# Dilated projections: 13 of 18 weight pieces as seven products of half blocks, state space tables in steps between

## The chip, the cores and the metric

The kernel runs on one core of a Trainium2 chip. The metric is the device time of one execution in microseconds, as the median of several runs. All arithmetic that is spoken of here is in f32.

## The reference

Four layers on 256 tokens of 1024 columns. The first two (attention with 256 context tokens, then attention on a grid, each with a mixture of 32 experts) are not touched. The third is dilated attention with 16 heads of 64, in three groups of different window and dilation, the fourth a grouped state space layer. What the change touches is the product `h @ w_in` of the third layer:

```python
def dilated_attention_mixer(h, w_in, w_out, rel_bias):
    B, S, _ = h.shape                       # 1, 256
    proj = h @ w_in                         # 1024 x (3*3*1024 + 1024)
    n_qkv = 3 * N_GROUPS_A * ATTN_WIDTH
    qkv = proj[..., :n_qkv].reshape(B, S, 3, N_GROUPS_A, ATTN_HEADS, HEAD_DIM)
    z = proj[..., n_qkv:]
    for g, (window, dilation) in enumerate(DILATED_GROUPS):
        o, l = dilated_group_attention(qkv[:, :, 0, g], qkv[:, :, 1, g], qkv[:, :, 2, g],
                                       rel_bias, window, dilation)
    ...
    return (o * jax.nn.silu(z)) @ w_out
```

The fourth layer's decays exp(A dt), their powers and a table of cosines and sines over 64 steps are computed on the chip from small inputs; these are the "state space tables".

## The kernel before

Every engine has a program of its own, in a fixed order written out by hand, and they meet on semaphores only: `ev(kind, ...)` is a signal, `at(kind, ...)` a wait for it, `vstep` a VectorE instruction that the next one waits for. The sync engine (SP) streams the weights through a ring of slots in SBUF, in the third layer three slots of 2 MB. A slot is loaded again when the last product that reads it has ended.

The heads are done in two halves, `hh` 0 and 1. Each half has nine weight pieces of 1024x512, `("dil", hh, g, c)`, for the groups g = 0, 1, 2 and c = 0 (Q), 1 (K), 2 (V). They are cut into parts, listed in `DIL`. A part of Q or K is one block of 128 output columns for all 256 tokens: 8 matmuls with a 128x128 block of the weight standing and 256 tokens moving, which leaves the result transposed (columns on the partitions). A part of V is one block of 128 tokens: 8 matmuls with the tokens standing and 512 weight columns moving. A half has 30 parts; n = 0 to 3 are (0, Q), 4 to 7 (0, K), and so on. The last two (n = 28, 29, the V piece of group 2) and the first six of the other half run between the attention steps of `pe_pairs`.

Around them: `pe_dil_part` (L2655) writes part n into PSUM bank n % 4. `act_dil_part` copies it to SBUF (L2680 for Q with the scale 0.125, L2682 for K, L2684 for V). In the second half VectorE copies K (L2691). `act_dil` runs ScalarE's parts, and after part 3 of the first half `act_tables` (exp, exp, sine, cosine on 128x32, L2527 to L2533). VectorE does, during the first half, all of `dve_tables`: L2549 and L2550, the wrapping of the angle in `dve_wrapped` (L2537 to L2544, twice), then small instructions on 128x32 (L2555 to L2618), and the table of angles, doubled from 1 to 64 (L2580 to L2585), on 32 to 1024 columns. `dve_outputs_begin` (L2937 to L2942, six instructions of 128x1024) runs after part 7 of the second half. GpSimd does eight masks `BM` of 128x768 before each half's attention (L2825); in the first half they wait for the constant `DM`, which ScalarE's queue loads (L2795). `pe_power_rows` turns the powers for a later load. `dil_done` is the wait of every engine for the last copies, and then come the attention steps (`pe_pairs`, `act_pairs`, `dve_pairs`, `pool_pairs`).

Three other places serve as measures in the rows below: `pe_keep` (L533) multiplies the identity by itself, 128 columns moving, just to keep TensorE at work; L2159 is a turn by matmul, with 128x128 blocks of the stream standing and 128 columns moving; L2858 is GpSimd's gate product on 128x256.

## Time and profile before

| | |
|---|---|
| median of 3 runs | 2081.4 us (2079.29 to 2089.8) |
| span of the profiled execution | 2082.8 us |
| TensorE busy | 1934.9 us, 93% |
| VectorE busy | 652.8 us, 31% |
| ScalarE busy | 364.7 us, 18% |
| GpSimd busy | 322.1 us, 15% |
| L2666 (Q and K parts) | 768 records of 128x256, 168.0 us |
| L2668 (V parts) | 192 records of 128x512, 84.1 us |

Times in a trace are microseconds from the start of the span. A record is one TensorE instruction; an f32 matmul of the program is two of them. PE is TensorE's matmuls and PEld its weight loads, which run beside them; DVE is VectorE, ACT ScalarE, POOL GpSimd. "Busy" of TensorE is the union of overlapping records, so the pace of a row of matmuls is read from the time between starts, not from the length of one. Idle time in brackets stands before the row, with the engine or DMA that ended it.

### The profile page before, as it was taken

What the parts mean: (1) busy time and instruction counts of PE and PEld (TensorE: products, weight loads), DVE (VectorE), ACT (ScalarE), POOL (GpSimd) and SP (SyncE); (2) the same over time, 40 slices, a digit from 0 to 9 for tenths busy, and PEclk for the clock granted to TensorE, in tenths of its full rate; (3) what the DMA queues carried; (4) which work ended last, traced back from release to release, by engine and by line L of the source; (5) the groups of instructions that cost most, each with busy time, mean ns of one, the idle gap of its engine ahead of it and who ended that gap; (6) DMA issues with size and microseconds to landing.
All of it is one profiled execution on the core that took longest, in us unless ns stands there. A gap on an engine that the chain in (4) does not pass through costs nothing.

```text
span 2082.8 us, 33820 instructions
## 1 busy us (share of the span) xinstructions
PE 1934.9 (93%) x14647; PEld 1203.4 (58%) x14647; DVE 652.8 (31%) x1517; ACT 364.7 (18%) x809; POOL 322.1 (15%) x264
## 2 busy tenths in 40 slices
PE   6989999999999989998999988888789999989998
PEld 4565566555555555546555444444376677675884
DVE  1343472222222242115421111111154131047752
ACT  3142410000000021213210000000020220042231
POOL 0143411000000100116110000000020060040120
PEclk9999999999999999999999999999999999999999
DMA  9694499999999988217599999999874414327221
GB/s 350 157 366 165 156 365 400 427 428 426 426 426 426 427 337 237 91 59 296 212 380 426 427 427 426 426 426 426 363 276 160 157 49 161 121 82 203 82 93 61
DMA packets 136109, 590.93 MB, mean 284 GB/s; under 512 B 19410, under 2 KB 35818, under 8 KB 111248
## 3 DMA queue, kind: packets, MB, share of 16 engines
q1 hardware_dynamic: 119536, 564.45, 68.7%
q10 hardware_dynamic: 10304, 17.83, 2.7%
q0 software_dynamic: 6112, 6.39, 0.9%
q8 instruction: 118, 1.93, 0.4%
q14 instruction: 39, 0.32, 0.0%
HBM read 576.95 MB, written 25.33 MB: 289 GB/s over the span
## 4 chain that ended last, share of the span: by engine, by line
PE 67%; DMA 22%; DVE 4%; issue 3%; POOL 2%; ACT 2%; SPq 0%; DVEq 0%; POOLq 0%; ACTq 0%
DMA RG<-in_moe_w 20%; PE banks L1594 13%; PE banks L2666 8%; PE banks L1619 6%; PE banks L1139 4%; PE banks L2261 4%; PE banks L2668 4%; PE banks L1570 4%; PE banks L2263 3%; PE banks L2867 3%; PE banks L3078 2%; PE banks L712 2%; DMA mods_rows<-AR 2%; PE banks L355 2%; POOL AR L957 1%
## 5 line engine op out<-in xcount | busy, mean ns | idle before, releaser
L1594 PE MATMUL banks<-RG,HT 128*64 128x256 f32 x3616 | 426.5, 389 | 35.9 <-DMA RG<-in_moe_w 33.2
L1594 PEld LDWEIGHTS banks<-RG,HT 128*64 128x64 f32 x3616 | 252.0, 134 | 222.1 <-DMA RG<-in_moe_w 56.2
L1873 POOL DMA_INDIRECT y_rows<-AR x64 | 63.9, 998 | 838.3 <-DVE AR L1633 809.9
L1603 DVE TENSOR_TENSOR AR<-AR,banks 128x256 f32<-128x256 f32 x64 | 38.6, 603 | 479.4 <-ACT AR L1599 428.2
L1619 PE MATMUL banks<-RG,AR 128*64 128x512 f32 x752 | 171.7, 598 | 3.1 <-DVE AR L1612 3.1
L2666 PE MATMUL banks<-HT,RG 128*128 128x256 f32 x768 | 168.0, 380 | 0.8 <-ACT HT L550 0.8
L2666 PEld LDWEIGHTS banks<-HT,RG 128*128 128x128 f32 x768 | 145.4, 190 | 22.8 <-issue 2.4
L1599 ACT ACTIVATE AR<-banks 128x256 f32<-128x256 f32 x64 | 24.6, 384 | 742.3 <-PE banks L1594 742.3
L1570 PE MATMUL banks<-AR 128*128 128x256 bf16 (+1 forms) x1152 | 149.3, 277 | 1.6 <-DVE AR L1558 1.5
L1570 PEld LDWEIGHTS banks<-AR 128*128 128x128 bf16 x1152 | 108.2, 98 | 33.3 <-issue 18.3
L1619 PEld LDWEIGHTS banks<-RG,AR 128*64 128x64 f32 x752 | 49.8, 136 | 93.8 <-issue 83.6
L1139 PE MATMUL banks<-RG,HT 128*128 128x512 f32 x192 | 87.5, 617 | 4.8 <-DVE AR L405 3.0
L2261 PE MATMUL banks<-HT,RG 128*128 128x256 f32 (+1 forms) x256 | 85.3, 489 | 3.2 <-ACT HT L2181 1.3
L2668 PE MATMUL banks<-RG,HT 128*128 128x512 f32 x192 | 84.1, 594 | 0.0
L957 POOL TENSOR_SCALAR AR<-AR,ST 128x768 f32<-128x768 f32 (+1 forms) x24 | 45.0, 1886 | 242.5 <-DVE ST L935 242.4
L957 POOL TENSOR_SCALAR AR<-AR,SVT 128x512 f32<-128x512 f32 x27 | 42.0, 1566 | 190.3 <-DVE SVT L935 190.3
L2261 PEld LDWEIGHTS banks<-HT,RG 128*128 128x128 f32 x256 | 47.7, 190 | 40.7 <-issue 35.6
L1139 PEld LDWEIGHTS banks<-RG,HT 128*128 128x128 f32 x192 | 37.8, 199 | 51.8 <-issue 51.8
L1583 ACT ACTIVATE HT<-banks 128x256 f32<-128x256 f32 x128 | 49.1, 384 | 106.2 <-PE banks L1570 105.1
L355 PE MATMUL banks<-RG,SC 128*32 128x128 f32 x1536 | 51.1, 291 | 15.2 <-DMA RG<-in_ada_w 15.2
L1594 PE MATMUL banks<-AR,HT 128*64 128x256 f32 x480 | 59.1, 398 | 6.5 <-DMA AR<-in_moe_w 6.5
L878 PE MATMUL banks<-IDN,AR 128*128 128x128 f32 x348 | 52.2, 284 | 11.8 <-POOL AR L957 9.4
(487 smaller groups left out, 2381.3 us busy)
## 6 DMA issues: line engine op xcount, KB each, us to landing
RG<-in_moe_w SPq DMA_DIRECT2D x160, 2048.0 KB, 23.4
AR<-in_moe_w SPq DMA_DIRECT2D x32, 2048.0 KB, 14.5
RG<-in_ada_w SPq DMA_DIRECT2D x24, 2048.0 KB, 10.7
RG<-in_attn_w_in SPq DMA_DIRECT2D x20, 2048.0 KB, 7.7
RG<-in_odd_w_in SPq DMA_DIRECT2D x6, 2048.0 KB, 19.7
RG<-in_ssm_w_in SPq DMA_DIRECT2D x4, 2048.0 KB, 8.8
AR<-y_rows SPq DMA_DIRECT2D x12, 512.0 KB, 6.0
RG<-in_even_w_out SPq DMA_DIRECT2D x2, 2048.0 KB, 12.3
```

Source lines behind the costliest of these rows:

```text
L355: m = pe.matmul(q[32 * j:32 * j + 32, :], SC[:, k, :], w[:, k, 128 * j:128 * j + 128], start=k == 0, stop=k == 7, skip_group_check=True)
L957: g.tensor_scalar(u["pb"][x], u["pb"][x], A.small_of(s, 3)[:, x:x + 1], None, MUL).then_inc(*ev("weighed_pool", name, s, x))
L1139: m = pe.matmul(PS[b], HT[:, k, 128 * t:128 * t + 128], w[:, k, :], start=k == 0, stop=k == 7)
L1570: m = pe.matmul(p, E.HB[t][:, i, k, :], E.one_hot(g, t), start=t == 0 and i == 0, stop=t == E.nt - 1 and i == 2)
L1594: m = pe.matmul(p[64 * h:64 * h + 64, 256 * i:256 * i + 256], x[:, k, :], w[:, h, k], start=k == 0, stop=k == 7, skip_group_check=True)
L1619: m = pe.matmul(q[64 * h:64 * h + 64, :], x, w2[:, i, 512 * h:512 * h + 512], start=i == 0, stop=i == 3)
L1873: g.indirect_dma_start(y, off, E.Y[b], None, bounds_check=2047, oob_is_err=False).then_inc(*event)
L2261: m = pe.matmul(p[:, 0:wd], w[:, k, 128 * j:128 * j + 128], HT[:, k, 0:wd], start=k == 0, stop=k == 7)
L2263: m = pe.matmul(p, HT[:, k, 128 * j:128 * j + 128], w[:, k, :], start=k == 0, stop=k == 7)
L2666: m = pe.matmul(p[:, 0:256], w[:, k, 128 * j:128 * j + 128], HT[:, k, 0:256], start=k == 0, stop=k == 7)
L2668: m = pe.matmul(p, HT[:, k, 128 * j:128 * j + 128], w[:, k, :], start=k == 0, stop=k == 7)
L2867: m = pe.matmul(PS[2 * h + t], src[:, k, 128 * t:128 * t + 128], w[:, k, :], start=k == 0, stop=k == 7)
```

## The change

13 of the 18 pieces (all but (0, Q) and (2, V) in the first half, and all but (0, Q), (0, K) and (2, V) in the second) are computed with seven products of half blocks in place of eight. The weight piece is cut into four blocks b11, b12, b21, b22 of 512x256 and the input into four of 128 tokens by 512. The sums of input blocks (`dve_seven_sums`, four instructions of 128x512 on VectorE) are made once per half. The sums of weight blocks are made for each piece, each one instruction on 128x1024, in place in the slot or in a scratch tile: GpSimd makes t3 = b22 - b12 and t2 = t3 + b11, VectorE makes t1 = b22 - t2 and t4 = b21 - t2. The products go to PSUM banks 0, 1 and 4. ScalarE copies the first product ("one") and writes one quarter of the output; VectorE makes u2 and u3 and writes the other three quarters ("22", "21", "12"), each reading a bank and a small tile, on 256 columns. A product of a Q or K piece is 8 matmuls with 128 tokens moving, one of a V piece 4 matmuls with 256 weight columns moving. The slot of the ring is free after the seventh product.

VectorE's tables are cut into 28 steps for the first half, one to seven instructions each, and 13 for the second; `dve_seven` takes one at four places of each piece. Up to the argument of the cosine they run as before, ahead of the first piece. `dve_outputs_begin` moves into the first half's steps, the doublings from 16 on into the second half. ScalarE's four table instructions stand one behind each of the parts 0 to 3. GpSimd's masks stand two behind each of the first four pieces. In the second half GpSimd starts after the last attention output of the first half.

```diff
+        def dil_seven(hh, g, c):
+
+            return (g, c) not in (((0, 0), (2, 2)), ((0, 0), (0, 1), (2, 2)))[hh]
...
-                    cols(("dil", hh, g, c), AW, c * 3072 + g * 1024 + hh * 512, 512, ("dil_in", hh, g, c, 3 if c < 2 else 1))
+                    cols(("dil", hh, g, c), AW, c * 3072 + g * 1024 + hh * 512, 512,
+                         ("seven", "dil", hh, g, c, 6) if dil_seven(hh, g, c) else ("dil_in", hh, g, c, 3 if c < 2 else 1))
...
+            def __init__(self, key, before, w, turned, banks, x, sums, t2, small, scale, outs):
+                self.key, self.before, self.turned, self.scale, self.outs = key, before, turned, scale, outs
+                self.b11, self.b12 = w[:, 0:4, 0:256], w[:, 0:4, 256:512]
+                self.b21, self.b22 = w[:, 4:8, 0:256], w[:, 4:8, 256:512]
+                self.banks = [PS[b][:, 0:256] for b in banks]
+                self.t2, (self.one, self.u2, self.u3) = t2, small
+                a, b, c = self.banks
+                self.products = ((a, x[0][0], self.b11, True), (b, sums[1], t2, True), (a, x[0][1], self.b21, False),
+                                 (b, sums[2], self.b12, False), (c, sums[0], self.b11, True), (b, x[1][1], self.b21, False),
+                                 (c, sums[3], self.b22, False))
...
+        def dve_seven_sums(v, key, x, sums):
+
+            s1, s2, s3, s4 = sums
+            v.tensor_tensor(s3, x[0][0], x[1][0], SUB)
+            vstep(v, v.tensor_tensor(s1, x[1][0], x[1][1], ADD))
+            vstep(v, v.tensor_tensor(s2, s1, x[0][0], SUB))
+            v.tensor_tensor(s4, x[0][1], s2, SUB).then_inc(*ev("seven_sums", *key))
+
+        def pe_seven_product(pe, Z, i):
+            q, x, w, first = Z.products[i]
+            for j in range(2 if Z.turned else 1):
+                for k in range(4):
+                    if Z.turned:
+                        m = pe.matmul(q[:, 128 * j:128 * j + 128], w[:, k, 128 * j:128 * j + 128], x[:, k, :],
+                                      start=first and j + k == 0, stop=k == 3, skip_group_check=True)
+                    else:
+                        m = pe.matmul(q, x[:, k, :], w[:, k, :], start=first and k == 0, stop=k == 3, skip_group_check=True)
+            m.then_inc(*ev("seven", *Z.key, i))
+
+        def pe_seven(pe, Z, landed_, sums):
+            pe.wait_ge(*landed_)
+            if Z.before is not None:
+                pe.wait_ge(*at("seven_11", *Z.before))
+            pe_seven_product(pe, Z, 0)
+            pe.wait_ge(*at("seven_sums", *sums))
+            pe.wait_ge(*at("seven_t2", *Z.key))
+            if Z.before is not None:
+                pe.wait_ge(*at("seven_21", *Z.before))
+            pe_seven_product(pe, Z, 1)
+            pe.wait_ge(*at("seven_one", *Z.key))
+            pe_seven_product(pe, Z, 2)
+            pe.wait_ge(*at("seven_u2", *Z.key))
+            pe_seven_product(pe, Z, 3)
+            pe.wait_ge(*at("seven_t1", *Z.key))
+            if Z.before is not None:
+                pe.wait_ge(*at("seven_12", *Z.before))
+            pe_seven_product(pe, Z, 4)
+            pe.wait_ge(*at("seven_t4", *Z.key))
+            pe.wait_ge(*at("seven_u3", *Z.key))
+            pe_seven_product(pe, Z, 5)
+            pe.wait_ge(*at("seven_22", *Z.key))
+            pe_seven_product(pe, Z, 6)
+
+        def act_seven(act, Z):
+            act.wait_ge(*at("seven", *Z.key, 0))
+            if Z.before is not None:
+                act.wait_ge(*at("seven_21", *Z.before))
+            act.activation(Z.one, Z.banks[0], ACT.Copy, scale=Z.scale).then_inc(*ev("seven_one", *Z.key))
+            act.wait_ge(*at("seven", *Z.key, 2))
+            act.activation(Z.out(0, 0), Z.shaped(Z.banks[0]), ACT.Copy, scale=Z.scale).then_inc(*ev("seven_11", *Z.key))
+
+        def dve_seven(v, Z, fill):
+            a, b, c = Z.banks
+
+            def add(out, bank, u, event):
+                v.scalar_tensor_tensor(out=out, in0=bank, scalar=Z.scale, in1=u, op0=MUL, op1=ADD).then_inc(*ev(event, *Z.key))
+
+            next(fill, None)
+            v.wait_ge(*at("seven_t2", *Z.key))
+            v.wait_ge(*at("seven", *Z.key, 0))
+            v.tensor_tensor(Z.b11, Z.b22, Z.t2, SUB).then_inc(*ev("seven_t1", *Z.key))
+            v.wait_ge(*at("seven_one", *Z.key))
+            v.wait_ge(*at("seven", *Z.key, 1))
+            if Z.before is not None:
+                v.wait_ge(*at("seven_12", *Z.before))
+            add(Z.u2, b, Z.one, "seven_u2")
+            next(fill, None)
+            v.wait_ge(*at("seven", *Z.key, 2))
+            v.tensor_tensor(Z.b21, Z.b21, Z.t2, SUB).then_inc(*ev("seven_t4", *Z.key))
+            v.wait_ge(*at("seven", *Z.key, 3))
+            add(Z.u3, b, Z.one, "seven_u3")
+            next(fill, None)
+            v.wait_ge(*at("seven_u3", *Z.key))
+            v.wait_ge(*at("seven", *Z.key, 4))
+            add(Z.out(1, 1), Z.shaped(c), Z.shaped(Z.u3), "seven_22")
+            next(fill, None)
+            v.wait_ge(*at("seven", *Z.key, 5))
+            add(Z.out(1, 0), Z.shaped(b), Z.shaped(Z.one), "seven_21")
+            v.wait_ge(*at("seven", *Z.key, 6))
+            add(Z.out(0, 1), Z.shaped(c), Z.shaped(Z.u2), "seven_12")
+
+        def pool_seven(g, Z, landed_):
+            g.wait_ge(*landed_)
+            g.tensor_tensor(Z.b12, Z.b22, Z.b12, SUB).then_inc(*ev("seven_t3", *Z.key))
+            g.wait_ge(*at("seven_t3", *Z.key))
+            if Z.before is not None:
+                g.wait_ge(*at("seven_t4", *Z.before))
+            g.tensor_tensor(Z.t2, Z.b12, Z.b11, ADD).then_inc(*ev("seven_t2", *Z.key))
...
-        def act_tables(act):
-            act.wait_ge(*at("table_loads", 4))
-            act.activation(DT, LDT, ACT.Exp).then_inc(*ev("dt"))
-            act.wait_ge(*at("decay"))
-            act.activation(RR, V0, ACT.Exp).then_inc(*ev("radius"))
-            act.wait_ge(*at("sine_in"))
-            act.activation(SI_, V2, ACT.Sin).then_inc(*ev("sine"))
-            act.wait_ge(*at("cosine_in"))
-            act.activation(CO, V0, ACT.Sin).then_inc(*ev("cosine"))
+        def act_table(act, i):
+            if i == 0:
+                act.wait_ge(*at("table_loads", 4))
+                act.activation(DT, LDT, ACT.Exp).then_inc(*ev("dt"))
...
+        def dve_tables_rest(v):
+
             v.wait_ge(*at("cosine"))
...
             vstep(v, v.tensor_tensor(G1, AIM, AIM, MUL))
+            yield
             vstep(v, v.tensor_tensor(G0, G0, G1, ADD))
             vstep(v, v.reciprocal(G0, G0))
...
+            yield from dve_outputs_begin(v)
+            v.memset(RC[:, :, 0:1], 1.0)
+            vstep(v, v.memset(RS[:, :, 0:1], 0.0))
...
+        def dve_angles(v, s, end, once):
+
+            while s < end:
+                c, d = bc(PC, 2, s), bc(PSN, 2, s)
+                x0, y0 = RC[:, :, 0:s], RS[:, :, 0:s]
+                x1, y1 = RC[:, :, s:2 * s], RS[:, :, s:2 * s]
+                w = XS[:, 3, :].rearrange("p (a b) -> p a b", a=32)[:, :, 0:s]
+                steps = ((x1, x0, c, MUL), (w, y0, d, MUL), (x1, x1, w, SUB), (y1, x0, d, MUL), (w, y0, c, MUL), (y1, y1, w, ADD))
+                for i, (o, a, b, op) in enumerate(steps):
+                    ins = v.tensor_tensor(o, a, b, op)
+                    if 2 * s == 64 and i == 5:
+                        ins.then_inc(*ev("angles"))
+                        v.wait_ge(*at("angles"))
+                    else:
+                        vstep(v, ins)
+                    if (i + 1) % once(s) == 0:
+                        yield
+                s *= 2
+                if s < 64:
+                    dve_squared(v, PC, PSN, PC, PSN)
+                    yield
...
         DIL_EARLY, DIL_LATE = 6, 28
+        DIL_X = [[HT[:, 4 * kh:4 * kh + 4, 128 * t:128 * t + 128] for kh in range(2)] for t in range(2)]
+        DIL_SUMS = [ar(3 * KK + 512 * i, 4, 128) for i in range(4)]
+        DIL_SMALL = [ar(5 * KK + 256 * i, 256) for i in range(3)]
+
+        def dil_sevens(hh):
+            pieces, before = [], None
+            for g in range(3):
+                for c in range(3):
+                    if dil_seven(hh, g, c):
+                        if c == 2:
+                            outs = [[V3[:, t, g, 256 * b:256 * b + 256] for b in range(2)] for t in range(2)]
+                        else:
+                            o = Q3[g] if c == 0 else K3[:, g]
+                            outs = [[o[:, 2 * b:2 * b + 2, 128 * t:128 * t + 128] for b in range(2)] for t in range(2)]
+                        key = "dil", hh, g, c
+                        pieces.append(Seven(key, before, where[key][0], c < 2, (0, 1, 4), DIL_X, DIL_SUMS, ar(2 * KK, 4, 256),
+                                            DIL_SMALL, 0.125 if c == 0 else 1.0, outs))
+                        before = key
+            return pieces
+
+        SEVENS = [dil_sevens(hh) for hh in range(2)]
...
-            if (g, c, j) == (0, 2, 0) and hh:
-                act.wait_ge(*at("att_out", "dil0", 7))
...
+        def dil_plain(hh):
+
+            return range(DIL_EARLY, 8) if hh else range(4)
+
         def act_dil(act, hh):
-            for n in range(DIL_EARLY if hh else 0, DIL_LATE):
+            for n in dil_plain(hh):
                 act_dil_part(act, hh, n)
-                if hh == 0 and n == 3:
-                    act_tables(act)
+                if hh == 0:
+                    act_table(act, n)
+            if hh:
+                act.wait_ge(*at("att_out", "dil0", 7))
+            for Z in SEVENS[hh]:
+                act_seven(act, Z)
+
+        def dve_dil(v, hh):
+            v.wait_ge(*at("turned_out", "dil", 1, 1))
+            dve_seven_sums(v, ("dil", hh), DIL_X, DIL_SUMS)
+            if hh == 0:
+                dve_tables(v)
+                fill = chain(dve_tables_rest(v), dve_angles(v, 1, 16, lambda s: 2 if s == 8 else 3))
+            else:
+                for n in dil_plain(hh):
+                    dve_dil_part(v, hh, n)
+                fill = dve_angles(v, 16, 64, lambda s: 1)
+            for Z in SEVENS[hh]:
+                dve_seven(v, Z, fill)
+            run(fill)
+
+        def pool_dil(g, hh):
+            masks = iter(range(8))
+            if hh:
+                g.wait_ge(*at("att_out", "dil0", 7))
+            for Z in SEVENS[hh]:
+                pool_seven(g, Z, landed(Z.key))
+                for h in islice(masks, 2):
+                    pool_mask(g, hh, h)
+            for h in masks:
+                pool_mask(g, hh, h)
 
         def dil_done(e, hh):
 
-            e.wait_ge(*at("dil_out_act", hh, 2, 0, 3))
-            e.wait_ge(*at(*dil_out(hh, 2, 1, 3)))
+            e.wait_ge(*at("seven_11", "dil", hh, 2, 1))
+            e.wait_ge(*at("seven_12", "dil", hh, 2, 1))
...
-                for n in range(DIL_EARLY if hh else 0, DIL_LATE):
+                for n in dil_plain(hh):
                     pe_dil_part(pe, hh, n)
+                for n in (4, 5) if hh else (0, 1):
+                    pe.wait_ge(*at(*dil_out(hh, *DIL[n])))
+                for Z in SEVENS[hh]:
...
         def dve_dilated(v):
             dve_final(v)
-            dve_tables(v)
             for hh in range(2):
-                if hh:
-                    for n in range(DIL_EARLY, DIL_LATE):
-                        dve_dil_part(v, hh, n)
-                        if n == 7:
-                            dve_outputs_begin(v)
+                dve_dil(v, hh)
                 dil_done(v, hh)
...
+        def pool_mask(g, hh, h):
+            g.tensor_tensor(BM[:, h], bc(BI[:, 8 * hh + h, :], 1, 3), DM, ADD).then_inc(*ev("mask", hh, h))
+
         def pool_dilated(g):
+            g.wait_ge(*at("turned_out", "dil", 1, 1))
             g.wait_ge(*at("mask_load"))
             g.wait_ge(*at("dist_rows", 1))
             g.wait_ge(*at("finished", 1))
             for hh in range(2):
                 if hh:
                     g.wait_ge(*at("shift", "dil0", 7))
-                for h in range(8):
-                    g.tensor_tensor(BM[:, h], bc(BI[:, 8 * hh + h, :], 1, 3), DM, ADD).then_inc(*ev("mask", hh, h))
+                pool_dil(g, hh)
                 pool_pairs(g, A2[hh], iter(()))
...
-            t1, t2 = ar(2 * KK, 32, 32), ar(3 * KK, 32, 32)
+            t1, t2 = [XS[:, i, :].rearrange("p (a b) -> p a b", a=32) for i in (2, 3)]
             v.wait_ge(*at("matrix_loads", 3))
             cr, ci = bc(CR, 2, 32), bc(CI, 2, 32)
+            yield
             v.tensor_tensor(t1, C2R, ci, MUL)
+            yield
             vstep(v, v.tensor_tensor(t2, C2N, ci, MUL))
```

In `act_table(act, i)` the four instructions of `act_tables` are the same, one for each i. `dve_tables` ends where the cosine's argument is ready.

## Rows read from the trace of the kernel before

**Rows 1.** The page: engines by busy time, and the slices.

```profile
PE 1934.9 (93%) x14647; PEld 1203.4 (58%) x14647; DVE 652.8 (31%) x1517; ACT 364.7 (18%) x809; POOL 322.1 (15%) x264
...
PEclk9999999999999999999999999999999999999999
```

**Rows 2.** The chain in order of time: start us, us, what ran.

```profile
1532.56 27.89 PE banks L2666 x128
...
1643.21 0.39 ACT AR L2682
...
1721.66 13.73 PE banks L2668 x32
...
1776.76 27.64 PE banks L2666 x128
```

**Rows 3.** Timeline, TensorE, 755 to 793: start us, us, engine, line, operation, shapes.

```profile
758.58 8.20 PE L533 MATMUL banks<-IDN 128*128 128x128 f32 x72
...
785.04 3.73 PE L2159 MATMUL banks<-AR,XS 128*128 128x128 f32 x32
```

**Rows 4.** Timeline, ScalarE, 1539 to 1556.

```profile
1539.77 0.38 ACT L2680 ACTIVATE HT<-banks 128x256 f32<-128x256 f32 x1 [2.85 <-PE banks L2666]
...
1554.55 0.23 ACT L2531 ACTIVATE SVT<-SVT 128x32 f32<-128x32 f32 x1 [3.09 <-DVE SVT L2544]
```

**Rows 5.** Timeline, VectorE, 1530 to 1640.

```profile
1548.70 1.20 DVE L2549 TENSOR_TENSOR SVT<-SVT 128x32 f32<-128x32 f32 x1 [18.50 <-ACT SVT L2527]
1549.82 1.84 DVE L2550 TENSOR_TENSOR SVT<-SVT 128x32 f32<-128x32 f32 x1
1551.70 1.72 DVE L2537 TENSOR_SCALAR SVT<-SVT 128x32 f32<-128x32 f32 x1
1553.46 0.18 DVE L2538 CAST SVT<-SVT 128x32 int32<-128x32 f32 x1
...
1583.05 1.22 DVE L2580 TENSOR_TENSOR RG<-RG,SVT 128x1024 f32<-128x1024 f32 x1
```

**Rows 6.** Groups by form, VectorE: count, busy us, mean ns, idle before.

```profile
L1603 DVE TENSOR_TENSOR AR<-AR,banks 128x256 f32<-128x256 f32 x64 | 38.6, 603 | 479.4 <-ACT AR L1599 428.2 <-issue 51.2
```

**Rows 7.** Timeline, GpSimd, from 1535; the masks alone in short windows.

```profile
1539.22 14.16 POOL L2825 TENSOR_TENSOR AR<-AR 128x768 f32<-128x768 f32 x8 [39.10 <-DMA AR<-in_k_dm]
...
1549.82 1.80 POOL L2825 TENSOR_TENSOR AR<-AR 128x768 f32<-128x768 f32 x1
...
1551.58 1.80 POOL L2825 TENSOR_TENSOR AR<-AR 128x768 f32<-128x768 f32 x1
```

**Rows 8.** Groups by form, GpSimd.

```profile
L574 POOL TENSOR_TENSOR AR<-AR 128x1024 f32<-128x1024 f32 x1 | 2.4, 2353 | 1.5 <-DVE AR L561 1.5
```

**Rows 9.** Timeline, VectorE and GpSimd together, 1824 to 1878.

```profile
1824.75 5.61 POOL L957 TENSOR_SCALAR AR<-AR,ST 128x768 f32<-128x768 f32 x3 [6.66 <-DVE ST L935]
...
1826.12 0.97 DVE L928 CUSTOM_DVE_ANT_0 banks<-banks,AR 128x768 f32<-128x768 f32 x1 [1.15 <-PE banks L850]
...
1870.53 0.73 POOL L2858 TENSOR_TENSOR XS<-XS,AR 128x256 f32<-128x256 f32 x1 [4.67 <-ACT AR L2851]
...
1875.64 1.44 POOL L2858 TENSOR_TENSOR XS<-XS,AR 128x256 f32<-128x256 f32 x1 [4.38 <-ACT AR L2851]
1876.52 1.63 DVE L2952 TENSOR_TENSOR AR<-AR 128x1024 f32<-128x1024 f32 x1
```

**Rows 10.** Windows: length us, busy and count by engine, granted clock, DMA share, GB/s.

```profile
1516.00:1518.00 2.00, 0.00 (x0) 0.00 (x0) 1.97 (x2) 0.00 (x0) 0.00 (x0) 1.00 1.03 393
1518.00:1519.60 1.60, 0.00 (x0) 0.00 (x0) 1.56 (x3) 1.15 (x2) 0.00 (x0) 0.50 1.05 389
...
1524.00:1526.00 2.00, 2.00 (x16) 2.00 (x15) 1.56 (x8) 0.77 (x3) 0.00 (x0) 0.79 1.08 366
```

**Rows 11.** Timeline, TensorE, 1495 to 1521.

```profile
1519.66 1.65 PE L533 MATMUL banks<-IDN 128*128 128x128 f32 x6 [5.74 <-DVE AR L2503]
```

**Rows 12.** The page: DMA issues: count, KB each, us to landing.

```profile
RG<-in_attn_w_in SPq DMA_DIRECT2D x20, 2048.0 KB, 7.7
```

83 lines of the change are left out of this document (47 added, 36 removed).

## The prediction

> **What bounds the kernel now.** I read the page first, then the chain of waits in order of time, then single engines in short windows. The page says that TensorE is busy for 93% of the span, at the full granted clock in every slice [rows 1]. The chain through the changed stage shows one thing only: from 1532.56 on it is the projection matmuls of L2666 and L2668, piece after piece with nothing between, to 1643.21 in the first half of the heads and from 1721.66 to 1804.40 in the second [rows 2]. TensorE's own time per piece is therefore on the path at full price, and so is every wait that is put into it. No row shows the chain on VectorE, ScalarE or GpSimd there; their work hides under 111 and 83 us of matmuls. What the reader should see besides is that this cover is now spent twice: the seven-product scheme makes VectorE and GpSimd work inside each piece, with TensorE waiting for them seven times a piece.
>
> **TensorE's part.** An f32 matmul is two records in the trace. Two Q/K pieces are 128 records of 256 columns in 27.64 us, 215.9 ns each, so a piece is 64 records, 13.82 us; a V piece is 32 records of 512 columns in 13.73 [rows 2]. After, a Q/K piece is 7 products of 8 matmuls, 112 records, but of 128 columns only. Their price is that of rows with the same shape, a fresh 128x128 load for each: L533 does 72 in 8.20 us and L2159 does 32 in 3.73; less the last one's 0.27 that is 7.93/71 = 111.7 and 3.46/31 = 111.6 ns [rows 3]. So 112 x 111.6 = 12.50 us, 1.32 less. It is not half of 215.9 (12.09), and I take the row. A V piece is 7 x 4 matmuls of 256 columns, 56 records x 215.9 = 12.09 us, 1.64 less. Of the 13 pieces 9 are Q or K (five in the first half of the heads) and 4 are V: 9 x 1.32 + 4 x 1.64 = 18.4 us off the path, if nothing waits. One product is 1.79 us (Q/K) or 1.73 (V).
>
> **What the product chain asks of the others.** One product's result reaches ScalarE or VectorE 0.30 us after its last record's slot (two parts of 16 records at 215.9 ns from 1532.56 end at 1539.47, the copy of the second begins at 1539.77 [rows 4]). In a piece VectorE runs, in this order: a table step, t1 (128x1024), u2, a table step, t4 (128x1024), u3, a table step, "22", a table step, "21", "12". A 128x1024 tensor_tensor is 1.22 us; the five with a PSUM input have 256 columns, and I take 0.50 for each, under the 0.60 of L1603, whose second input is in PSUM (at 0.60 the sum is 1.5 higher) [rows 6]. GpSimd runs t3 and t2 (128x1024), then two masks. A mask is 1.77 on average (8 in 14.16), and a 128x1024 there is 2.35, in proportion to the mask's 768 columns [rows 7, 8]. Alone, this all fits: VectorE has 2.4 + 2.5 us of own work and four table steps of about 1.1 each (five steps of 32 columns at 0.225 apart), 9.3 of 12.5 us; each of TensorE's waits is met with some 1 us in hand; GpSimd has 8.2 of 12.5. The end of a half gains 0.3 us of tail, because the last product is followed by a VectorE add instead of a 0.39 us copy. That sum is -18.4 + 0.3 = about -18.
>
> **But they don't run side by side.** This is where I chose. In the trace of before the first table steps meet the masks. Three VectorE instructions of 32 columns, whose fellows take 0.18, took 1.20, 1.84 and 1.72 us, and each ended within 0.1 us of the end of a mask instruction (one starts at 1549.82, one at 1551.58, the last ends at 1553.38); from 1553.46, with GpSimd idle, they are 0.18 again [rows 5, 7]. So a VectorE instruction waits for the whole GpSimd instruction, and only one gets in between two of them, although the second was ready. It holds the other way too: L2858 takes 1.44 in place of 0.73 where a 128x1024 of VectorE runs, and VectorE's next, at 1876.52, takes 1.63 in place of 1.22 [rows 9]. With an input in PSUM VectorE is not held: L928, 768 columns, takes 0.97 inside GpSimd's three from 1824.75 [rows 9], about a column a nanosecond and no more. Thus u2, u3, "22", "21", "12" are free of it; t1, t4, the four sums and all table steps are not.
> The Trainium skill (SBUF — State Buffer, "Who interferes with whom") says the same and adds that whoever starts first keeps the shared ports for its whole instruction; had the page a bandwidth split instead, the steps of 32 columns would cost next to nothing and the sum would be the -18. The rows here side with the lock.
>
> Walk through a piece with this rule. After t4, GpSimd's t2 of the next piece is released and it runs t2, mask, mask, t3 without a gap: 2.35 + 2 x 1.77 + 2.35 = 8.2 us. VectorE's third table step stands between u3 and "22". If it is five small instructions, they get in one by one between those four, so "22" ends 8.2 + 0.5 + 0.3 us or so after t4's end. TensorE wants "22" for the seventh product two products and a half after t4, about 3 us. The stall is near 6 us. That meets pieces one and two of the first half (6.4, 6.0) and piece two of the second (6.0), whose third step is a squaring of five. Where the third step is one or two instructions it is 0 to 2.4. Laid out with the same rule for all of them, TensorE waits 3.1 (below) + 0.8 + 6.4 in piece one, 6.0 in two, 0.5 in three, 2.0 + 1.3 in four, 2.4 in five, 0.2 in six: 22.7 us. In the second half, where the steps are mostly single instructions of 512 or 1024 columns: 0.6, 6.9, 0.5, 2.1, together 10.1. The 3.1: the masks' data land at 1539.22 [rows 7], GpSimd then runs t3, t2, two masks and t3 until 1549.8, and the 16 wrapping steps behind "dt" crawl; the sine on ScalarE waits for them, and ScalarE's fourth part copy, the cosine and the copy "one" are queued behind that sine. In before the sine comes as late as 1554.55, but with 27.6 us of cover from the next piece [rows 4].
> Sum: -18.4 + 0.3 + 22.7 + 10.1 = **+14.7 us**. With 128x1024 on GpSimd a tenth shorter it is +9.6, a tenth longer +20.
>
> **The clock.** Before L533 TensorE is idle for 5.74 us, to 1519.66 [rows 11]. The granted clock is still 1.00 from 1516 to 1518 and 0.50, which is 1.2 of 2.4 GHz, from 1518 on; over 1524 to 1526 it averages 0.79, so it is back at 1524.84, 5.2 us after work begins [rows 10]. Each such fall costs half of 5.2, 2.6 us. I have three stalls of 6.0 to 6.4 us, just longer than the idle that brought it down, so 0 to 7.8 us; I take half, 3.9.
> Forecast: 2082.8 + 14.7 + 3.9 = 2101.4 for the profiled execution. The median of the runs is 1.4 below the profiled span, so **2100.0 us**, 0.9% slower.
>
> **What costs nothing.** The angle tables are wanted only in the state space stage, past 1950; the powers by power rows at the end of the first half, and they are in the second piece's steps. Weight pieces of 2 MB land 7.7 us after issue [rows 12] and there are three slots, so a piece in 12 to 20 us starves nobody. Moving ScalarE's wait for the last attention output ahead of the V pieces delays only copies that come later anyway. The masks come later than now, yet are done by the fourth piece, before the attention. Four sums of 512 columns (0.69 each) run at 1532.5, before the first seven-product piece at 1546.4.
>
> **Rivals.** (1) *The lock does not bind*: small instructions slip through, TensorE's waits stay met, 2082.8 - 18.1 - 1.4 = **2063**, 0.9% faster. The price is the 18.4 of fewer columns; it decides as long as the third table step ends before the sixth product. For it speaks that only three instructions were seen held; against it that all three were held to the end. 17%. (2) *Half of it*: the lock is there but the meeting is rarer (GpSimd held back by VectorE's own instructions, a second small one getting in, 2.1 us instructions), so the stalls are 10 to 27 us instead of 33, with no fall of the clock: **2073 to 2091**, within 0.5%. 20%. (3) *Narrow matmuls slower than L2159's*: if the recorded load of 0.19 us were the pace at 128 columns, a Q/K piece were 21.3 us, 67 us more in all, 2150 or above. L533 and L2159 speak against it. 3%. The forecast with its stalls has 60%: 2092 to 2112.
>
> **How the numbers follow.** The range for 8 in 10 leaves out rival 1 and rival 3: 2070 to 2112; the likeliest case alone is 2092 to 2112. 0.5% (10.4 us) is about what a measurement of this kernel can tell. Faster 0.19 (rival 1 and the edge of 2), same 0.19, slower 0.62 (forecast and rival 3).
>
> **What would show it.** In the changed kernel: products of 16 records in 1.79 and 1.73 us (else the first term is wrong); table steps of 32 columns at 1.8 to 2.4 us while GpSimd works (else the lock is); TensorE idle 6 us before the seventh product, released by "22", in the first two pieces; a ScalarE sine late enough to hold "one"; a clock of 0.50 in slices behind these idles. If TensorE is gapless there, rival 1 holds and I am wrong by 36 us; if the gaps are there but half as long, my count of meetings is wrong.

## The result and the profile after

The changed kernel took **2099.77 us** (median; 2096.05 to 2108.01, 5 runs) against 2081.88 of the kernel before in the same comparison (2079.29 to 2089.8, 5 runs). The ratio is 1.0078, with a 95% interval of 1.0052 to 1.0104: about 0.8% slower. The profiled execution has a span of 2099.7 us; 2082.8 was that of before.

The page of the changed kernel (busy us, share of the span, instructions; then the granted clock by slices):

```profile
PE 1924.4 (92%) x15175; PEld 1230.0 (59%) x15175; DVE 766.3 (36%) x1608; ACT 359.0 (17%) x799; POOL 392.5 (19%) x290
...
PEclk9999999999999999999999999999989999999999
```

Beside [rows 1] TensorE is busy for 10.5 us less, VectorE for 113.5 us more and GpSimd for 70.4 more. The span grew all the same, so TensorE must be waiting, and one slice shows a lower clock. Where it is can be read from two windows for each kernel: the first half of the heads, from the first projection matmul to the first attention product, and the second half, from the group of 48 projection matmuls to the first attention product behind them. TensorE alone; columns: window, length, busy (records), granted clock, DMA share, GB/s. Before:

```profile
1532.56:1643.74 111.18, 110.83 (x451) 1.00 0.47 168
1711.04:1804.99 93.95, 93.34 (x370) 1.00 0.38 135
```

After, and below them short windows around the stalls:

```profile
1535.38:1659.96 124.58, 107.88 (x738) 0.95 0.42 147
1727.25:1823.13 95.88, 87.67 (x610) 0.98 0.38 133
...
1566.00:1572.00 6.00, 3.90 (x17) 0.50 0.00 0
1580.00:1590.00 10.00, 4.95 (x19) 0.81 0.00 0
```

The two halves take 220.5 us instead of 205.1, 15.3 more. That is nearly the whole of the 16.9 by which the spans differ: another 2.8 lie ahead of the stage, where both kernels do the same work and profiled executions differ by several us, and the rest of the kernel gives 1.2 back. In the first half TensorE is idle for 16.7 us (124.58 less 107.88), where it was idle for 0.35.

TensorE's timeline in the first two pieces and around the one long stall of the second half:

```profile
1554.20 2.05 PE L1002 MATMUL banks<-HT,RG 128*128 128x128 f32 x16 [1.16 <-ACT AR L1036]
...
1560.31 1.95 PE L1002 MATMUL banks<-HT,RG 128*128 128x128 f32 x16
1568.10 3.78 PE L1002 MATMUL banks<-AR,RG 128*128 128x128 f32 x16 [5.84 <-DVE AR L1044]
...
1587.68 3.78 PE L1005 MATMUL banks<-RG,AR 128*128 128x256 f32 x8 [5.05 <-DVE AR L1044]
...
1593.89 1.95 PE L1002 MATMUL banks<-AR 128*128 128x128 f32 x16
1595.68 1.95 PE L1002 MATMUL banks<-HT,RG 128*128 128x128 f32 x16
...
1767.33 3.56 PE L1002 MATMUL banks<-AR,RG 128*128 128x128 f32 x16 [5.14 <-DVE HT L1044]
```

Before, the rows were unbroken [rows 2]. Here products follow one another in 1.79 us only where nothing disturbs them (1593.89 to 1595.68). The seventh product of pieces one and two (L1002 and L1005) waits 5.84 and 5.05 us for VectorE's "22" (L1044), then runs in 3.78 us instead of about 2, at half the clock. What VectorE did in the first of these stalls:

```profile
1558.92 0.42 DVE L1044 SCALAR_TENSOR_TENSOR AR<-banks,AR 128x256 f32<-128x256 f32 x1
1559.25 2.29 DVE L2690 TENSOR_TENSOR SVT<-SVT 128x32 f32<-128x32 f32 x1
1561.58 1.72 DVE L2691 TENSOR_TENSOR SVT<-SVT 128x32 f32<-128x32 f32 x1
1563.34 1.73 DVE L2692 TENSOR_TENSOR SVT<-SVT 128x32 f32<-128x32 f32 x1
1565.10 2.26 DVE L2693 TENSOR_TENSOR SVT<-SVT 128x32 f32<-128x32 f32 x1
1567.40 0.19 DVE L2694 TENSOR_TENSOR SVT<-SVT 128x32 f32<-128x32 f32 x1
1567.62 0.42 DVE L1044 SCALAR_TENSOR_TENSOR AR<-banks,AR 128x256 f32<-128x256 f32 x1
```

and GpSimd in the same time (t2 L1076, two masks L3000, t3 L1072):

```profile
1559.15 2.35 POOL L1076 TENSOR_TENSOR AR<-RG 128x1024 f32<-128x1024 f32 x1 [6.67 <-DVE RG L1057]
1561.46 3.56 POOL L3000 TENSOR_TENSOR AR<-AR 128x768 f32<-128x768 f32 x2
1564.97 2.34 POOL L1072 TENSOR_TENSOR RG<-RG 128x1024 f32<-128x1024 f32 x1
```

Four additions of 32 columns take as long as GpSimd's four instructions, one each, and end as those end; the fifth takes 0.19 us, GpSimd being done. The same happened to three instructions before the change [rows 5, 7], where nobody waited.

### The profile page after: what moved, and what is told of

Read it like the earlier page. It is cut to its first block, busy times and chain, and to the rows that moved or that the text cites. A ratio compares the mean times of both kernels' runs of the same rounds, so it can differ in the third digit from the quotient of the medians.

```text
span 2099.7 us, 35070 instructions
## 1 busy us (share of the span) xinstructions
PE 1924.4 (92%) x15175; PEld 1230.0 (59%) x15175; DVE 766.3 (36%) x1608; ACT 359.0 (17%) x799; POOL 392.5 (19%) x290
## 4 chain that ended last, share of the span: by engine, by line
PE 62%; DMA 22%; DVE 8%; issue 3%; POOL 2%; ACT 2%; ACTq 0%; SPq 0%; DVEq 0%; POOLq 0%
DMA RG<-in_moe_w 20%; PE banks L1710 12%; PE banks L1735 5%; PE banks L1002 4%; PE banks L1255 4%; PE banks L2377 4%; PE banks L1686 3%; PE banks L2379 3%; PE banks L3052 3%; PE banks L3270 2%; PE banks L719 2%; DMA mods_rows<-AR 2%; PE banks L1005 2%; POOL AR L964 1%; PE banks L661 1%
## 5 line engine op out<-in xcount | busy, mean ns | idle before, releaser
L1686 PEld LDWEIGHTS banks<-AR 128*128 128x128 bf16 x1152 | 108.4, 98 | 33.6 <-issue 18.3
L1255 PE MATMUL banks<-RG,HT 128*128 128x512 f32 x192 | 86.1, 609 | 4.8 <-DVE AR L412 3.0
L2377 PEld LDWEIGHTS banks<-HT,RG 128*128 128x128 f32 x256 | 47.7, 190 | 40.7 <-issue 35.6
L1002 PE MATMUL banks<-AR,RG 128*128 128x128 f32 x432 | 55.3, 287 | 13.7 <-DVE AR L1044 8.5
L1749 DVE TENSOR_TENSOR AR<-banks,XS 128x512 f32<-128x512 f32 x32 | 22.1, 691 | 115.3 <-PE banks L1735 115.3
L1735 PE MATMUL banks<-AR 128*64 128x512 f32 x272 | 62.1, 598 | 1.0 <-DVE AR L1728 1.0
L1002 PEld LDWEIGHTS banks<-AR,RG 128*128 128x128 f32 x432 | 52.8, 202 | 15.2 <-DVE AR L1044 9.7
```

The lines of the kernel that those rows point to most:

```text
L1002: m = pe.matmul(q[:, 128 * j:128 * j + 128], w[:, k, 128 * j:128 * j + 128], x[:, k, :], start=first and j + k == 0, stop=k == 3, skip_gro ...
L1255: m = pe.matmul(PS[b], HT[:, k, 128 * t:128 * t + 128], w[:, k, :], start=k == 0, stop=k == 7)
L1686: m = pe.matmul(p, E.HB[t][:, i, k, :], E.one_hot(g, t), start=t == 0 and i == 0, stop=t == E.nt - 1 and i == 2)
L1735: m = pe.matmul(q[64 * h:64 * h + 64, :], x, w2[:, i, 512 * h:512 * h + 512], start=i == 0, stop=i == 3)
L2377: m = pe.matmul(p[:, 0:wd], w[:, k, 128 * j:128 * j + 128], HT[:, k, 0:wd], start=k == 0, stop=k == 7)
```

## The experiments

The theory, **by turns**: VectorE and GpSimd instructions that both work in SBUF don't run side by side; a small one waits for the whole large one, one for each. The third table step of a piece meets GpSimd's stretch, holds "22", and with it TensorE. The rival, **load**: with the combinations of the scheme and the table steps, VectorE simply has more to do between two products than fits. A second rival came up later, **place**: a step between u3 and "22" is too much there, whatever GpSimd does.

Times are against the kernel before in the same comparison (medians there 2080.8 to 2084.4). Because profiled executions differ by several us ahead of the stage (it starts between 1527 and 1538), the surer measure is the length of the two halves, read as above, from one profiled execution of each kernel:

| kernel | first half | second | sum | median us | ratio, 95% |
|---|---|---|---|---|---|
| before | 111.2 | 94.0 | 205.1 | | 1 |
| changed | 124.6 | 95.9 | 220.5 | 2099.8 | 1.0052 to 1.0104 |
| masks_twice | 128.1 | 99.2 | 227.2 | 2109.3 | 1.0112 to 1.0148 |
| third_step_behind_22 | 117.1 | 94.6 | 211.6 | 2093.5 | 1.0026 to 1.006 |
| keep_clock | 122.1 | 94.4 | 216.5 | 2093.8 | 1.0026 to 1.0064 |
| masks_late | 120.8 | 89.6 | 210.4 | 2087.8 | 1.0 to 1.0031 |
| steps_last | 113.3 | 86.5 | 199.8 | 2084.8 | 0.9998 to 1.003 |
| weight_sums_only | 121.3 | 98.8 | 220.0 | 2092.5 | 1.003 to 1.0068 |
| weight_sums_masks_moved | 105.1 | 86.9 | 192.0 | 2070.0 | 0.9902 to 0.9949 |
| weight_sums_on_vectore | 103.9 | 86.3 | 190.1 | 2070.2 | 0.991 to 0.9947 |
| one_mask_per_piece | 101.4 | 85.4 | 186.8 | 2064.2 | 0.9888 to 0.9934 |

**masks_twice**: more of GpSimd's work, with nothing more for VectorE.

```diff
                 for h in islice(masks, 2):
+                    gstep(g, g.tensor_tensor(BM[:, h], bc(BI[:, 8 * hh + h, :], 1, 3), DM, ADD))
                     pool_mask(g, hh, h)
```

> The changed kernel with each of GpSimd's eight masks per half made twice (the first copy feeds nobody); VectorE's and TensorE's programs are untouched. If VectorE's instructions wait for whole GpSimd instructions (the lock), the stretch behind t4 grows from t2, mask, mask, t3 = 8.2 us to t2, four masks, t3 = 11.8 us, and the five-instruction third steps meet five of them in place of four: about 14 us more than the changed kernel, near 2114 us. If TensorE waits only because VectorE has too much of its own to do, nothing changes, since GpSimd is idle for 7 to 12 us in each piece: 2100 us.

Measured: 6.7 us more in the two halves than the changed kernel, half of the 14 expected. A new stall of 4.72 us came up (the third product, for the copy "one"), and the three stalls behind "22" became shorter, not longer: 4.29, 2.99 and 4.33 us, which the theory as it stood did not say. VectorE's third step of piece one, and GpSimd beside it (L2878 the added copies):

```profile
1563.58 1.51 DVE L2690 TENSOR_TENSOR SVT<-SVT 128x32 f32<-128x32 f32 x1
1565.12 1.73 DVE L2691 TENSOR_TENSOR SVT<-SVT 128x32 f32<-128x32 f32 x1
1566.89 0.19 DVE L2692 TENSOR_TENSOR SVT<-SVT 128x32 f32<-128x32 f32 x1
1567.11 1.68 DVE L2693 TENSOR_TENSOR SVT<-SVT 128x32 f32<-128x32 f32 x1
```

```profile
1565.00 1.81 POOL L2878 TENSOR_TENSOR AR<-AR 128x768 f32<-128x768 f32 x1
1566.88 1.86 POOL L3001 TENSOR_TENSOR AR<-AR 128x768 f32<-128x768 f32 x1
1568.70 1.80 POOL L2878 TENSOR_TENSOR AR<-AR 128x768 f32<-128x768 f32 x1
```

A second small instruction (L2692) gets in at 1566.89, where GpSimd has waited for the end of its own added copy before it starts the mask (from about 1566.81 to 1566.88). The step also began later, with GpSimd's t2 already under way, so that its first addition was held for 1.51 us and not 2.29. Load says 2100 and is out; the rule needs the correction that such a gap on GpSimd lets a second small one through.

**third_step_behind_22**: the third step's place alone.

```diff
             add(Z.u3, b, Z.one, "seven_u3")
-            next(fill, None)
             v.wait_ge(*at("seven_u3", *Z.key))
             v.wait_ge(*at("seven", *Z.key, 4))
             add(Z.out(1, 1), Z.shaped(c), Z.shaped(Z.u3), "seven_22")
             next(fill, None)
+            next(fill, None)
```

> The changed kernel with VectorE's third table step of each piece behind the addition 22 in place of ahead of it; the work of every engine is the same. If the place in VectorE's queue is what turns a held table step into an idle TensorE, the 6 us idles ahead of the seventh product go, and smaller ones (about 4 us, behind 21, which the next piece's second product wants) take their place: laid out with the same rule it is 13 us less, about 2087 us. If the amount of work or of lock time is what counts, it stays at 2100 us.

Measured: 8.9 us less in the two halves, 6.3 less in the median, where 13 were expected. The same four additions (L2690 to L2693) now take 0.62, 1.73, 1.73 and 2.27 us behind "22", and hold "21" instead, on which the next piece's second product waits: 3.75 and 2.85 us of idle in the first half, 3.16 in the second. The clock still fell behind them (the product after the first of these waits took 2.52 us and the next 3.07 in place of 1.89). The hold went on, only its victim changed.

**keep_clock**: the price of the clock by itself. TensorE multiplies the identity ahead of the seventh product in the three pieces with a long stall; nothing reads the result.

```diff
+            if Z.key[1:] in ((0, 0, 1), (0, 0, 2), (1, 1, 0)):
+                pe_keep(pe, 16, 5)
             pe.wait_ge(*at("seven_22", *Z.key))
             pe_seven_product(pe, Z, 6)
```

> The changed kernel with 16 dummy matmuls (3.6 us of 128 columns, into a bank that nobody reads) ahead of the seventh product of the three pieces in which TensorE idles for more than 5 us. The idle is there anyway, so the dummies cost nothing. If the half clock behind these idles is worth what the trace of the changed kernel shows (the seventh product takes 3.8, 3.8 and 3.4 us in place of 1.8), the granted clock stays at 1.00 and the time falls by 5 to 7 us, to about 2094 us. If the clock is absorbed by the waits that come after, it stays at 2100 us.

Measured: 4.0 us less in the two halves, 6.0 in the median. In windows:

```profile
1567.00:1568.00 1.00, 0.00 (x0) 0.94 0.00 0
1568.00:1569.00 1.00, 0.83 (x4) 0.50 0.00 0
...
1580.00:1590.00 10.00, 8.50 (x60) 1.00 0.01 2
```

Two of the three falls are gone (1580 to 1590 has 1.00 in place of 0.81). In piece one only 2.29 us of idle are left and the clock still falls, just before the product comes (0.94 over 1567 to 1568). So two of the three falls were worth 4 to 6 us of the loss, and the stalls are the rest.

**weight_sums_on_vectore**: t3 and t2 of the next piece go from GpSimd to VectorE, the step between u3 and "22" goes behind "21", and GpSimd's masks wait for the sixth product.

```diff
             v.tensor_tensor(Z.b21, Z.b21, Z.t2, SUB).then_inc(*ev("seven_t4", *Z.key))
+            if after is not None:
+                dve_seven_first(v, after)
             v.wait_ge(*at("seven", *Z.key, 3))
             add(Z.u3, b, Z.one, "seven_u3")
-            next(fill, None)
+            if after is not None:
+                dve_seven_second(v, after)
...
             add(Z.out(1, 0), Z.shaped(b), Z.shaped(Z.one), "seven_21")
+            next(fill, None)
...
-                pool_seven(g, Z, landed(Z.key))
-                for h in islice(masks, 2):
+                g.wait_ge(*at("seven", *Z.key, 5))
+                for h in islice(masks, 2 if Z.before is None or hh and Z.key[2:] == (1, 0) else 1):
```

> All four sums of weight blocks on VectorE (t3 and t2 of the next piece stand behind t4 and u3), no table step between u3 and 22 but one behind 21, and GpSimd makes only the masks, one behind the sixth product of each piece (two in the first, and in the first two of the second half). VectorE gets 2 x 1.22 us more per piece, GpSimd loses 4.7 us. If the lock is the cause, TensorE is nearly gapless in the pieces and the whole gain of the seven products comes out: 2082 - 18 = 2064 us, and 2070 at most. If VectorE's load is the cause, it gets worse: 13 pieces with 2.4 us more each, above 2105 us.

Measured: 2070.2 us, at the upper end of what the theory gave, and faster than both kernels. VectorE does **more** in each piece than in the changed kernel (two sums of 1.22 us) and the stalls of 5 us are gone. Load is out for good. But three things were moved at once, so two more kernels take them apart, below.

**masks_late**: the masks alone, moved behind the last piece's t2.

```diff
                 pool_seven(g, Z, landed(Z.key))
-                for h in islice(masks, 2):
-                    pool_mask(g, hh, h)
```

> GpSimd makes its eight mask copies of a half only behind the weight sums t3 and t2 of the half's last piece, instead of two behind each piece's. Lock theory (a table step of four or five instructions on VectorE moves on by one instruction for each instruction of GpSimd): GpSimd's stretch behind t4 shrinks from t2, two masks, t3 (8.2 us) to t2 and t3 (4.7 us), so the third steps of pieces one and two of the first half and of piece one of the second, that held TensorE 5.84, 5.05 and 5.14 us, hold it some 1.5 to 2.5 us each; the clock stays up, and the time is about 2087 (2083 to 2091). In the last piece of a half the masks lie beside VectorE instead, for 0 to 3 us. Load theory (VectorE has more to do in a piece than fits behind its products, whatever GpSimd does): the stalls stay at 5 us each and the time at 2100.

Measured: 2087.8, within a us of the expected 2087. VectorE, third step of piece one, with t2 and t3 alone beside it, and "22" and the start of the fourth step of the last piece but one, beside eight masks without a gap:

```profile
1554.88 2.29 DVE L2690 TENSOR_TENSOR SVT<-SVT 128x32 f32<-128x32 f32 x1
1557.20 2.26 DVE L2691 TENSOR_TENSOR SVT<-SVT 128x32 f32<-128x32 f32 x1
1559.50 0.19 DVE L2692 TENSOR_TENSOR SVT<-SVT 128x32 f32<-128x32 f32 x1
...
1631.48 0.42 DVE L1044 SCALAR_TENSOR_TENSOR AR<-banks,AR 128x256 f32<-128x256 f32 x1
1631.82 1.34 DVE L2745 TENSOR_TENSOR SVT<-SVT 128x32 f32<-128x32 f32 x1
1633.19 1.73 DVE L2746 TENSOR_TENSOR SVT<-SVT 128x32 f32<-128x32 f32 x1
```

```profile
1627.63 14.29 POOL L2998 TENSOR_TENSOR AR<-AR 128x768 f32<-128x768 f32 x8
```

Two of five are held where GpSimd has two instructions, and all five where its masks go on past them (TensorE then waits 5.00 us). Each is held until the instruction it meets is done: 2.3 us for 1024 columns, 1.73 for 768. The addition with an operand in PSUM (L1044) takes its 0.42 in the midst of the masks. The stalls at the three seventh products in question (that of the second half is in its piece two, where the expectation has piece one) were 2.72, 1.99 and 1.88 us, about the 1.5 to 2.5 expected. Two things were not as expected. Beside the masks at the end of the first half TensorE waited 2.75 and 5.00 us, where I gave 0 to 3 in all. And the clock did not stay up: it fell behind the 1.99, the 1.88 and the 5.00. The time is hit more closely than its parts.

**steps_last**: no table step inside the pieces.

```diff
@@ dve_seven, in all four places @@
-            next(fill, None)
```

> VectorE runs no table step inside the pieces; all steps of a half follow its last piece. Both theories say that the stalls of 5 to 6 us inside the pieces go (the steps are what is held or what is too much), and that the pieces come at the pace of their products, 12.5 us a piece of Q or K and 12.1 us a piece of V: the first half's pieces then take about 106 us instead of 124. What they differ in is the whole: under the lock theory the steps behind the last piece run at their own pace (0.2 us an instruction of 32 columns, 1.2 to 1.8 us the larger ones) but for the masks still under way, in all some 20 us a half, and those of them that the next stage waits for stand on the path: 2090 to 2105 as a whole. Under the load theory the steps take as long there as they did inside the pieces, and the whole is above 2110. The reading is the pace of the pieces and the duration of the small instructions of 32 columns by the trace, not the time alone.

Measured: the pieces run at 12.5 and 12.1 us but for waits of 1.56 and 2.19 in the first, and the second half takes 86.5 us. The steps then stand on the path. TensorE and VectorE at the first half's end:

```profile
1645.15 0.48 PE L2750 MATMUL banks<-IDN,SVT 128*128 128x128 f32 x1 [7.62 <-DVE SVT L2704]
...
1669.69 0.58 PE L857 MATMUL banks<-AR,HT 64*128 64x128 f32 x2 [4.75 <-ACT AR L917]
```

```profile
1644.91 0.19 DVE L2704 TENSOR_TENSOR SVT<-SVT 128x32 f32<-128x32 f32 x1
```

Beside an idle GpSimd every one of these additions takes 0.17 to 0.19 us. The whole, 2084.8, is a little under the 2090 I gave as its lower end. The first half's steps run from 1637.92 to 1666.99, 29 us and not the 20 I gave, but only 7.62 us of them and, in the attention, 4.75 were waited for.

**weight_sums_only**: the weight sums on VectorE, but the step back between u3 and "22" (behind t2), and two masks a piece from t4 on.

```diff
@@ against weight_sums_on_vectore @@
                 dve_seven_second(v, after)
+            next(fill, None)
...
             add(Z.out(1, 0), Z.shaped(b), Z.shaped(Z.one), "seven_21")
-            next(fill, None)
...
-                g.wait_ge(*at("seven", *Z.key, 5))
-                for h in islice(masks, 2 if Z.before is None or hh and Z.key[2:] == (1, 0) else 1):
+                g.wait_ge(*at("seven_t4", *Z.key))
+                for h in islice(masks, 2):
```

> Of the kernel with the weight sums on VectorE (2070.2) the sums alone: t3 and t2 of the next piece on VectorE behind t4 and u3, but the table steps stay where the changed kernel has them (between u3 and 22 too, now behind t2) and GpSimd makes two masks a piece from t4 on, beside that third step. Lock theory: GpSimd's stretch behind t4 is two copies (3.6 us) instead of four instructions (8.2 us), of which VectorE's t3, u3 and t2 (2.9 us) already cover a part, so a third step loses at most two instructions to it (under 3.6 us, some 1 to 2 us behind 22): no stall above 3 us, the clock stays up, 2072 (2068 to 2078). Load theory: VectorE gets 2.44 us more in each piece with all its steps in place, so the stalls grow and the time is above 2105. A third reading, that the stalls came from where the steps stood and not from GpSimd, gives 2094 or more, since moving the step alone gave 2093.5.

Measured: 2092.5, a clear miss: by the two halves (220.0) the move of the sums gained nothing at all. (The median lies lower than the changed kernel's. In the profiled execution the first projection starts at 1527.25, 8.1 us earlier, though the work ahead of it is the same; why, and whether it is so in the other executions, stays open.) By the time alone, "place" would be right, which gave 2094. The trace says otherwise. VectorE, t2 and the first two additions of the step in piece one, and then t2 and its step in piece five, when all masks are done:

```profile
1549.41 2.50 DVE L1048 TENSOR_TENSOR AR<-RG 128x1024 f32<-128x1024 f32 x1
1551.83 1.78 DVE L2697 TENSOR_TENSOR SVT<-SVT 128x32 f32<-128x32 f32 x1
1553.65 0.19 DVE L2698 TENSOR_TENSOR SVT<-SVT 128x32 f32<-128x32 f32 x1
...
1618.28 1.22 DVE L1048 TENSOR_TENSOR AR<-RG 128x1024 f32<-128x1024 f32 x1
1619.41 0.22 DVE L2737 TENSOR_TENSOR RG<-RG,SVT 128x64 f32<-128x64 f32 x1
```

GpSimd's two masks of piece one:

```profile
1548.20 5.37 POOL L3009 TENSOR_TENSOR AR<-AR 128x768 f32<-128x768 f32 x2 [52.95 <-DVE RG L1067]
```

The sum t2 of 1024 columns takes 2.50 us instead of 1.22, and the two masks 5.37 instead of 3.56: they are done in turn, first mask, t2, second mask, and then only the step's first addition. I had let VectorE's large sums cover a part of the masks; but large ones don't cover each other, they queue. In the first half TensorE waited 2.99, 2.96, 3.04 and 3.12 us in the four pieces with masks and then 0.20 and nothing in the pieces without, with the step in the same place. The first two of these waits:

```profile
1555.04 2.05 PE L1002 MATMUL banks<-AR,RG 128*128 128x128 f32 x16 [2.99 <-DVE AR L1054]
...
1570.41 3.56 PE L1005 MATMUL banks<-RG,AR 128*128 128x256 f32 x8 [2.96 <-DVE AR L1054]
```

The second product runs in 3.56 us in place of 1.99, at half the clock. The expectation had the clock staying up; it fell behind five of the seven waits of about 3 us in the two halves, and by the products' starts that cost some 9.6 us.

**weight_sums_masks_moved**: the kernel just above, with the masks behind the sixth product, and nothing else changed.

```diff
@@ against weight_sums_only @@
-                g.wait_ge(*at("seven_t4", *Z.key))
-                for h in islice(masks, 2):
+                g.wait_ge(*at("seven", *Z.key, 5))
+                for h in islice(masks, 2 if Z.before is None or hh and Z.key[2:] == (1, 0) else 1):
```

> As the kernel with the weight sums alone on VectorE (2092.5, stalls of 2.96 to 3.12 us in the four pieces that have masks beside their third step, 0.2 and none in the pieces that have none), but GpSimd's masks wait for the sixth product of a piece, one a piece after the first. Its table steps stay between u3 and 22. By turns (each of GpSimd's instructions and each of VectorE's stand in each other's way): t2 takes 1.22 us again instead of 2.50 and the third step 1.1 us, so that no stall behind 22 is above 0.5 us, the clock stays at 2.4 GHz through the pieces, and the time is that of the kernel that moves the step as well, 2070 (2062 to 2074). Place of the step: if a step between u3 and 22, behind t2, is too much for VectorE by itself, the stalls of 3 us stay and the time at 2090.

Measured: 2070.0. The step is still between u3 and "22"; its row and t2's:

```profile
1558.84 1.22 DVE L1048 TENSOR_TENSOR AR<-RG 128x1024 f32<-128x1024 f32 x1
1559.97 0.18 DVE L2697 TENSOR_TENSOR SVT<-SVT 128x32 f32<-128x32 f32 x1
...
1561.76 1.75 DVE L2752 TENSOR_TENSOR SVT<-SVT 128x32 f32<-128x32 f32 x1
```

Nothing is held between t2 and "22" there; the two masks of the first piece, from 1561.67, now hold two additions of the step behind "22", 1.75 and 1.73 us, and TensorE waits 1.06 us once. Its next longest wait is 0.61 us, for "22" in the second half, a little over the 0.5 expected; the clock stays up. This pair differs only in when GpSimd makes its masks, and is 22.5 us apart (28.0 in the two halves): "place" falls, "by turns" stands.

**one_mask_per_piece**: weight_sums_on_vectore with a single mask in every piece, the last one behind the last piece, and no step behind the last piece's "21".

```diff
@@ against weight_sums_on_vectore @@
-                for h in islice(masks, 2 if Z.before is None or hh and Z.key[2:] == (1, 0) else 1):
+                for h in islice(masks, 1):
...
@@ dve_seven, behind "21" @@
-            next(fill, None)
+            if after is not None:
+                next(fill, None)
```

> As the kernel with the weight sums on VectorE (2070.2), but with one mask copy a piece throughout, the rest behind the last piece, and no table step between the quarters 21 and 12 of a half's last piece. Lock theory: what is left of holds near the masks (steps of 1.6 and 1.8 us in piece one) and at the end of a half (the tail's wait of 1.3 us) goes, so 1 to 2 us less: 2068.5 (2067 to 2071). A rival: the masks left over stand between the last piece and the attention that reads them, 1.8 us each for three of them, and the time is 2071 to 2075.

Measured: 2064.2 (2059.88 to 2066.6), the fastest of all, 0.9% under the kernel before. Windows of the two halves:

```profile
1698.76:1784.19 85.43, 84.82 (x610) 1.00 0.43 149
1530.95:1632.35 101.40, 101.01 (x739) 1.00 0.52 181
```

No idle beyond that of before, full clock throughout. It is 6.0 us under weight_sums_on_vectore where I gave 1 to 2; by the two halves it is 3.3, and the rest lies outside them, where executions differ by as much.

## Why the prediction was right, point by point

The forecast was 2100.0 us and the measurement 2099.77. The single steps were less exact than that.

- **TensorE's part** (18.4 us off the path, +0.3 of tail): right. Without stalls (one_mask_per_piece) the halves take 186.8 us in place of 205.1, 18.3 less, where 18.1 was predicted; in the first half its busy time went from 110.83 to 101.01, 9.8, where five times 1.32 and twice 1.64 make 9.9. A product of 16 records is 1.785 us, 111.6 ns a record, as the narrow rows of before had it.
- **By turns**: right in kind, in place and nearly in size. The three long stalls came in the pieces named, released by "22" as named, 5.84, 5.05 and 5.14 us for 6.4, 6.0 and 6.9. What the two halves take beyond those of one_mask_per_piece, less the clock (below), is 27.1 us of waits (18.3 and 8.8), where 22.7 and 10.1 were predicted. Two terms were oversized. The additions with an operand in PSUM take 0.42 us where I took 0.50. And the wait for "one" behind the sine was 1.16 us, not 3.1: of the wrapping steps two got in unheld. One (0.18 us at 1544.22) came where GpSimd had waited for its own t3 ahead of t2, as in masks_twice. The other (0.17 us at 1550.09) came where GpSimd goes from the masks to the next t3; VectorE starts it without waiting for the instruction ahead of it, but what let it in is not shown. The rule "one for one" was too strict there. (My "about a column a nanosecond" for L928 was a loose reading too: 768 columns in 0.97 us are 1.26 ns a column.) The Trainium skill (SBUF — State Buffer, "Who interferes with whom") says that the one that comes later is blocked for the whole instruction, which the held rows above bear out; that two large ones take turns is in the rows of weight_sums_only, and the page does not go so far.
- **The clock** (3.9 us of 0 to 7.8): undersized. It fell at all three long stalls, and at half the clock the three products and what follows them lost 2.2, 2.7 and 1.6 us, 6.5 in all by their starts; keep_clock, with two of the three gone, gives 4.0 to 6.0. My reason for taking half was wrong too: I held the stalls to be just about as long as the one idle time known to bring the clock down, 5.7 us. It falls after far shorter ones (1.99 us in masks_late).
- The two errors go in opposite directions: −5.7 of stalls, +2.6 of clock. The stage came out at +15.3 instead of +18.6. For the profiled execution the forecast was 2101.4, and 2099.7 came: 3.3 less in the stage, 2.8 more ahead of it (a difference of executions as far as the traces of the other kernels tell, not of the change), 1.2 less behind. The median then lay at the profiled span and not 1.4 below it, as I had taken. That the total was hit to a fraction of a us is luck.
- **Rivals**: that the hold doesn't bind, and half of it, both fall; narrow matmuls are as the rows of before said. **What costs nothing** held with one exception: the second half's activation sums, for which I gave 0.69 us each, met GpSimd's t2, masks and t3 and took 1.8 to 2.7, and held the first V piece there for 0.75.

## What to carry to other kernels

Before VectorE and GpSimd share a pipeline with deadlines, look in the trace for small VectorE instructions as long as the GpSimd instruction beside them. Their work adds up instead of overlapping: a step of five tiny instructions, harmless at 1.1 us, becomes as long as four or five of GpSimd's. It isn't the amount of work that must be moved but the meeting: giving GpSimd's sums to VectorE, which does one in 1.22 us instead of 2.35, and letting GpSimd work only where VectorE has slack, turned a change that cost 0.8% into one that gains 0.9%. The first of the two alone gained nothing (weight_sums_only), and GpSimd's masks moved alone gave back 10.1 us of the two halves (masks_late).
